# Four boundaries, the modulation sums and two early waits are rearranged in a two-block transformer kernel

## The reference

```python
# first block
x = x + 0.5 * swiglu(rmsnorm(x, ffn1_norm), ffn1_wgu, ffn1_wdown)          # f0
h = rmsnorm(x, mix_norm); z = h @ w_in
... # windowed attention, gated 31-tap causal convolution, merged, @ w_out
x = x + 0.5 * swiglu(rmsnorm(x, ffn2_norm), ffn2_wgu, ffn2_wdown)          # f1
e = rmsnorm(p @ ple_proj, ple_norm)
x = x + sigmoid(rmsnorm(x, ple_gate_norm) @ ple_gate_w) * e                # "gate", "emb"
# second block: nine modulation rows of 1024 from one vector c
mods = silu(c) @ w_ada + b_ada        # sh1, sc1, gt1, sh2, sc2, gt2, sh3, sc3, gt3
h = rmsnorm(x, g_pre[0]) * (1 + sc1) + sh1
x = x + 0.5 * gt1 * rmsnorm(swiglu(h, w_gu1, w_dn1), g_post[0])            # f2
h = rmsnorm(x, g_pre[1]) * (1 + sc2) + sh2
x = x + gt2 * rmsnorm(token_mixer(h), g_post[1])                           # mix2: GLA and forgetting attention
h = rmsnorm(x, g_pre[2]) * (1 + sc3) + sh3
x = x + 0.5 * gt3 * rmsnorm(swiglu(h, w_gu2, w_dn2), g_post[2])            # f3
```

## Time and profile before

| | |
|---|---|
| Time, median of 3 runs | 1416.35 us (1415.77 to 1418.84) |
| The profiled execution | 1407.82 us, its span 1406.0 us |
| Mean granted TensorE clock | 0.997 |
| PE busy | 1365.9 us, 97% of the span |
| DVE, ACT, POOL busy | 913.2, 742.9 and 57.8 us |

### The profile page before, as it was taken

One profiled execution on the slowest core, in us unless ns is written; L12 is line 12 of the kernel. 1 busy time (PEld: TensorE's weight loads), 2 busy tenths in 40 slices (PEclk: granted clock), 3 DMA queues, 4 the chain that ended last, 5 costly groups with the idle time before them and its releaser, 6 DMA issues.

```text
span 1406.0 us, 16993 instructions
## 1 busy us (share of the span) xinstructions
PE 1365.9 (97%) x6534; PEld 1127.1 (80%) x6534; DVE 913.2 (65%) x1309; ACT 742.9 (53%) x1144; POOL 57.8 (4%) x112
## 2 busy tenths in 40 slices
PE   7999999999999999999999999999999999899997
PEld 5888787878888888788688878688888888688886
DVE  5767747857466767666677774667776456755543
ACT  5544447556674544345754444766456563744442
POOL 3001000000000010000001000000000000000000
PEclk9999999999999999999999999999999999999999
DMA  9888756543257788765488875656453355456662
GB/s 296 280 264 279 224 177 187 175 130 91 90 179 237 224 275 275 268 216 159 145 259 270 266 247 174 184 153 177 143 156 91 105 162 170 147 180 187 188 184 85
DMA packets 166992, 270.68 MB, mean 193 GB/s; under 512 B 14178, under 2 KB 114698, under 8 KB 166912
## 3 DMA queue, kind: packets, MB, share of 16 engines
q1 hardware_dynamic: 154240, 226.66, 51.9%
q0 software_dynamic: 12368, 42.58, 9.1%
q10 hardware_dynamic: 304, 0.35, 0.1%
HBM read 268.50 MB, written 1.05 MB: 192 GB/s over the span
## 4 chain that ended last, share of the span: by engine, by line
PE 85%; DVE 5%; DMA 4%; ACT 4%; issue 1%; SPq 0%; DVEq 0%; ACTq 0%
PE ps L1769 26%; PE ps L1748 15%; PE ps L1750 15%; PE ps L1749 15%; DVE w_lo L1044 3%; DMA raw<-in_ffn_wgu_dram 2%; PE ps L1924 1%; ACT w_hi L573 1%; PE ps L2220 1%; DMA raw<-in_ffn_wdown_dram 1%; ACT shift L625 1%; PE ps L1836 1%; PE ps L1818 1%; PE ps L1960 1%; PE ps L1820 1%
## 5 line engine op out<-in xcount | busy, mean ns | idle before, releaser
L1044 DVE TENSOR_TENSOR w_lo<-raw,w_hi 128x1024 fp32r<-128x1024 f32 (+2 forms) x431 | 515.5, 1215 | 290.8 <-ACT w_hi L573 289.0
L573 ACT ACTIVATE w_hi<-raw 128x1024 fp32r<-128x1024 f32 (+2 forms) x431 | 447.8, 1054 | 334.4 <-DMA raw<-in_ffn_wgu_dram 95.1
L1748 PE MATMUL ps<-w_hi,a_hi 128*128 128x512 f32 (+1 forms) x1056 | 424.4, 402 | 1.9 <-DVE w_lo L1044 1.3
L1750 PE MATMUL ps<-w_hi,a_lo 128*128 128x512 f32 (+1 forms) x1056 | 411.9, 390 | 0.0
L1749 PE MATMUL ps<-w_lo,a_hi 128*128 128x512 f32 (+1 forms) x1056 | 411.1, 389 | 0.0
L1750 PEld LDWEIGHTS ps<-w_hi,a_lo 128*128 128x128 f32 x1056 | 199.1, 189 | 42.7
L1748 PEld LDWEIGHTS ps<-w_hi,a_hi 128*128 128x128 f32 x1056 | 199.5, 189 | 41.4 <-DVE w_lo L1044 2.7
L1749 PEld LDWEIGHTS ps<-w_lo,a_hi 128*128 128x128 f32 x1056 | 199.8, 189 | 37.8
L1769 PE MATMUL ps<-w_hi,hid_hi 128*128 128x512 f32 x336 | 105.1, 394 | 0.0
L1769 PE MATMUL ps<-w_lo,hid_hi 128*128 128x512 f32 x336 | 104.0, 391 | 0.0
L1769 PE MATMUL ps<-w_hi,hid_lo 128*128 128x512 f32 x336 | 104.0, 391 | 0.0
(11 more groups left out here) (380 smaller groups left out, 1389.8 us busy)
## 6 DMA issues: line engine op xcount, KB each, us to landing
raw<-in_ffn_wgu_dram SPq DMA_DIRECT2D x176, 256.0 KB, 4.4
raw<-in_w_in_dram SPq DMA_DIRECT2D x88, 512.0 KB, 3.7
raw<-in_w_gu_dram SPq DMA_DIRECT2D x176, 256.0 KB, 3.4
ada<-in_w_ada_dram POOLq DMA_DIRECT2D x72, 512.0 KB, 5.3
raw<-in_ffn_wdown_dram SPq DMA_DIRECT2D x44, 512.0 KB, 4.0
raw<-in_w_dn_dram SPq DMA_DIRECT2D x44, 512.0 KB, 3.6
raw<-in_w_in_dram SPq DMA_DIRECT2D x36, 256.0 KB, 3.0
raw<-in_w_out_dram SPq DMA_DIRECT2D x16, 512.0 KB, 3.5
```

Of the source, the lines that this page charges most:

```text
L573: act.activation(w_hi[:, u % RING, 0:nk * n], raw[:, u % RING, 0:nk * n], ACT.Copy).then_inc(hi_ready, 1)
L1044: dve.tensor_tensor(w_lo[:, u % RING, 0:nk * n], raw[:, u % RING, 0:nk * n], w_hi[:, u % RING, 0:nk * n].bitcast(F32), ALU.subtract).then_ ...
L1748: pe.matmul(dst(t)[:, 0:n], a[0], slot(u, w_hi, kk, n), start=kc == 0, stop=False)
L1750: i = pe.matmul(dst(t)[:, 0:n], a[1], slot(u, w_hi, kk, n), start=False, stop=kc == KC - 1)
```

## The change

- **Modulation sums.** DVE first transposes `acc_m` in blocks of 32x32 into two PSUM banks and reduces it to 128 x 32 (`fold_mods`, after blocks 4 and 8 of f0, f1 and f2); PE then makes one matmul of 32 columns with a new constant table (`C_SUM`) after the fourth unit of blocks 5 and 9. DVE takes the result one block later, in four pieces of 32 partitions.
- **Tile 0 at the boundaries.** POOL makes the high parts (`tile_hi` in its list), chunks 0 and 1 alone and then pairs; DVE makes the low parts of chunks 0 and 1 alone (`chunk_lo`). In tile 1 ACT makes the high parts of chunks 0 and 1 alone.
- **Second tile gated ahead.** At the boundaries to mix2 and f3 DVE does the two `gated` of tile 1 before the root of tile 0's norm, and ACT's square of tile 1 waits for them.
- **Boundary to f2.** Two weight units are split after the sigmoid of tile 0 instead of before it, on ACT and on DVE; the sum of tile 1 goes between low parts; `busy` has 10 matmuls instead of 20.
- **Last tile by halves.** The last two units of f3 are multiplied first into the one half of tile 1, then into the other; squares and gate products are made by halves.
- **Taps and GLA.** The last two tap matmuls move from step 10 to step 12. The 12 value matmuls of the GLA move into the middle of the next weight unit.

```diff
--- before.py
+++ after.py
...
-C_ID, C_ONES, C_TRI, C_D, C_W, C_COS, C_SIN, C_GLA = 0, 128, 256, 384, 512, 640, 656, 672
+C_ID, C_ONES, C_TRI, C_D, C_W, C_COS, C_SIN, C_SUM, C_GLA = 0, 128, 256, 384, 512, 640, 656, 672, 800
...
     s, q = i[:, None], i[None, :]
+    t[:, C_SUM:C_SUM + P] = s % 32 == q % 32
...
 epsb = keep("epsb", [P, 3])
+half_ss = keep("half_ss", [P, 2])
...
+    def tile_hi(key):
+        g = MODS[key]
+        for c, n in ((0, 1), (1, 1), (2, 2), (4, 2), (6, 2)):
+            pool.wait_ge(sem("shifted"), KC * T * g + c + n)
+            pool.tensor_copy(a_hi[:, c:c + n, 0:P], shift[:, c:c + n, :]).then_inc(sem("first_hi" if c == 0 else "act_hi"), 1)
...
     load_brow(2)
+    tile_hi("f2")
     load_ada(2 * ADA_F + 3, 3 * ADA_F)
+    tile_hi("mix2")
     pool.dma_start(ggla[:, :], A["g_gla_2"][0].partition_broadcast(P)).then_inc(sem("glam_landed"), 16)
+    tile_hi("f3")
...
                     act.activation(shift[:, k, :], turn_to(key, t, k), ACT.Identity, scale=modA[:, g, k:k + 1], bias=modB[:, g, k:k + 1])                               .then_inc(sem("shifted"), 1)
+                    if t == 1 and c == 0:
+                        act.wait_ge(sem("shifted"), KC * (T * g + t) + k + 1)
+                        act.activation(dst[:, k, :], shift[:, k, :], ACT.Copy).then_inc(sem("first_hi" if k == 0 else "act_hi"), 1)
+                if t == 0 or c == 0:
+                    continue
...
         act.wait_ge(used, end)
+        act.wait_ge(sem("post_made"), 4 * POST[prev])
...
     act.wait_ge(sem("rstd_ready"), NORM["gate"] + 1)
-    w.to(u_pg + KC + 2)
     act.activation(st[:, 0, 0, 0:T], rstd[:, :], ACT.Sigmoid)
+    w.to(u_pg + KC)
     act.activation(h[:, 0, :], behind(0), ACT.Sigmoid, scale=rstd[:, 0:1]).then_inc(sem("gate_ready"), 1)
+    w.to(u_pg + KC + 2)
...
     ffn_part(3)
-    for t in range(T):
...
-        post_tile("f3", t)
+    act.wait_ge(sem("first_tile"), FIRST_TILE["f3"])
+    post_tile("f3", 0)
+    act.wait_ge(sem("first_tile"), FIRST_TILE["f3"] + 1)
+    act.activation(junk[:, 0:512], acc(1, 0), ACT.Square, accum_out=half_ss[:, 0:1]).then_inc(sem("ss_ready"), 1)
+    act.wait_ge(used, ffn[3][1] + FC)
+    act.activation(junk[:, 512:], acc(1, 1), ACT.Square, accum_out=pss[:, 1:2]).then_inc(sem("pss_ready"), 1)
+    act.wait_ge(sem("pss_ready"), 2 * POST["f3"] + 2)
+    act.wait_ge(sem("emb_ready"), T + 1)
+    act.activation(rt[:, 1, 1:2], pss[:, 1:2], ACT.Sqrt, scale=1.0 / D, bias=half_ss[:, 1:2]).then_inc(sem("sqrt_ready"), 1)
...
+    def chunk_lo(key, t, c):
+        if c == 0:
+            dve.wait_ge(sem("first_hi"), T * MODS[key] + t + 1)
+        else:
+            dve.wait_ge(sem("act_hi"), 8 * TURN[key] + 4 * t + 1)
+        dst, hf = (v[:, c, t * P:(t + 1) * P] for v in (a_lo, a_hi))
+        dve.tensor_tensor(dst, shift[:, c, :], hf.bitcast(F32), ALU.subtract).then_inc(sem("first_lo" if c == 0 else "act_lo"), 1)
...
-    def post_and_norm(prev, key):
+    def post_and_norm(prev, key, end):
...
         post_sum(prev, 0, 1)
+        dve.wait_ge(used, end)
+        gated(prev, 1, 0)
+        gated(prev, 1, 1)
         normalise(key, 0)
-        dve.wait_ge(sem("pss_ready"), 2 * POST[prev] + 2)
-        gated(prev, 1, 0)
-        gated(prev, 1, 1)
-        tile_lo(key, 0, 0, 2)
         post_root(prev, 1)
+        chunk_lo(key, 0, 0)
+        post_sum(prev, 1, 0)
+        chunk_lo(key, 0, 1)
         tile_lo(key, 0, 2, 4)
-        post_sum(prev, 1, 0)
         normalise(key, 1)
-        tile_lo(key, 1)
+        chunk_lo(key, 1, 0)
+        chunk_lo(key, 1, 1)
+        tile_lo(key, 1, 2)
...
                 hidden_lo(f, j - 1)
-            take_mods(FFN[f], j)
+            take_mods(FFN[f], j - 1)
...
             i.then_inc(sem("hid_ready"), 1)
+            if f < 3 and j in (4, 8):
+                fold_mods(3 * f + j // 4 - 1)
...
+    def fold_mods(m):
+        dve.wait_ge(sem("ada_used"), KC * (m + 1))
+        blocks_ = ps[:, 6:8, :].rearrange("p b n -> p (b n)")
+        then(dve.transpose(blocks_, acc_m[:, m % 2, :]))
+        dve.tensor_reduce(rs36[:, 0:32], blocks_.rearrange("p (b n) -> p b n", n=32), AX, ALU.add).then_inc(sem("mod_folded"), 1)
...
             g, kind = m // 3, m % 3
-            if kind == 0:
...
+            if kind < 2:
+                for q in range(4):
+                    r = slice(32 * q, 32 * (q + 1))
+                    src = ps[r, 6, 0:32].rearrange("p (c q) -> p c q", q=4)[:, :, q]
+                    i = dve.tensor_tensor((modB, modA)[kind][r, g, :], src, par[r, :, ROW[("b_ada_2", m)]], ALU.add)
+            if kind == 1:
                 r = ROW[("g_pre_2", g)]
-                then(dve.tensor_tensor(modA[:, g, :], ps[:, 6, 0:KC], par[:, :, ROW[("b_ada_2", m)]], ALU.add))
+                then(i)
                 i = dve.scalar_tensor_tensor(modA[:, g, :], modA[:, g, :], 1.0, par[:, :, r], ALU.add, ALU.mult)
-            else:
+            elif kind == 2:
...
         dve.scalar_tensor_tensor(emb[:, t, :], wide(t), prs[:, t:t + 1], grow[:, :], ALU.mult, ALU.mult).then_inc(sem("emb_ready"), 1)
-    w.to(u_pg + KC + 2)
+    w.to(u_pg + KC)
         then(dve.tensor_tensor(h[:, t, :], h[:, t, :], emb[:, t, :], ALU.mult))
+    def emb_sum(t):
     gate_emb(0)
+    emb_sum(0)
+    w.to(u_pg + KC + 1)
     normalise("f2", 0)
-    tile_lo("f2", 0, 0, 2)
     gate_emb(1)
-    tile_lo("f2", 0, 2)
+    chunk_lo("f2", 0, 0)
+    chunk_lo("f2", 0, 1)
+    emb_sum(1)
+    tile_lo("f2", 0, 2, 4)
+    w.to(u_pg + KC + 2)
+    tile_lo("f2", 0, 4)
     normalise("f2", 1)
-    tile_lo("f2", 1)
+    chunk_lo("f2", 1, 0)
+    chunk_lo("f2", 1, 1)
+    tile_lo("f2", 1, 2)
     ffn_part(2)
-    post_and_norm("f2", "mix2")
+    post_and_norm("f2", "mix2", ffn[2][1] + FC)
...
     w.to(u_wo2 + KC + 2)
-    post_and_norm("mix2", "f3")
+    post_and_norm("mix2", "f3", u_wo2 + KC)
     ffn_part(3)
-    for t in range(T):
...
+    dve.wait_ge(sem("pss_ready"), 2 * POST["f3"] + 1)
+    gated("f3", 0, 0)
...
+    dve.wait_ge(sem("ss_ready"), 2 * len(NORM) + 1)
+    dve.tensor_scalar(half_ss[:, 1:2], half_ss[:, 0:1], 1.0 / D, EPS, ALU.mult, ALU.add).then_inc(sem("emb_ready"), 1)
+    gated("f3", 1, 0)
+    dve.wait_ge(sem("pss_ready"), 2 * POST["f3"] + 2)
+    gated("f3", 1, 1)
...
+    dve.wait_ge(sem("emb_ready"), T + 1)
+    then(dve.scalar_tensor_tensor(v, pss[:, 1:2], 1.0 / D, half_ss[:, 1:2], ALU.mult, ALU.add))
+    dve.wait_ge(sem("sqrt_ready"), ROOTS.index("f3_post1") + 1)
...
+    post_sum("f3", 1, 0)
+    post_sum("f3", 1, 1)
...
-    def last_rows(u0, n, hi, lo, bank=0, late=None):
+    def row_quarter(u, kc, t, half, last, hi, lo):
+        a = [v[:, kc, t * P:(t + 1) * P] for v in (hi, lo)]
+        for x_, w_ in ((0, w_hi), (0, w_lo), (1, w_hi)):
+            i = pe.matmul(acc(t, half), a[x_], slot(u, w_, 0, D, 512 * half, 512 * (half + 1)), start=False, stop=kc == last and x_ == 1)
+        return i
+    def last_rows(u0, n, hi, lo, bank=0, late=None, halves=False):
         i.then_inc(sem("first_tile"), 1)
+        if halves:
...
+            for half in range(2):
+                for k in range(n - 2, n):
+                    i = row_quarter(u0 + k, k, 1, half, n - 1, hi, lo)
+                    if half == 1:
+                        i.then_inc(used, 1)
+                if half == 0:
+                    i.then_inc(sem("first_tile"), 1)
+            return
...
         n = group(key)
-        pe.wait_ge(sem("act_lo"), 8 * TURN[key] + 4 * t + (kc // n + 1) * n // 2)
+        if key in MODS and kc == 0:
+            pe.wait_ge(sem("first_lo"), T * MODS[key] + t + 1)
+        else:
+            pe.wait_ge(sem("act_lo"), 8 * TURN[key] + 4 * t + (kc // n + 1) * n // 2)
...
                         turn_hidden(f, j - 1)
+                if i == 3:
...
         pe.wait_ge(sem("hid_lo_ready"), f * UPB + UPB)
-        last_rows(dn, FC, hid_hi, hid_lo, late=late)
+        last_rows(dn, FC, hid_hi, hid_lo, late=late, halves=f == 3)
...
             if m % 3 < 2:
-                pe.wait_ge(sem("ada_used"), KC * (m + 1))
+                pe.wait_ge(sem("mod_folded"), 2 * (m // 3) + m % 3 + 1)
...
             else:
-                for c in range(KC):
-                    i = pe.matmul(ps[:, 6, c:c + 1], acc_m[:, m % 2, c * P:(c + 1) * P], ones[:, 0:1], start=True, stop=True)
+                i = pe.matmul(ps[:, 6, 0:32], const[:, C_SUM:C_SUM + P], rs36[:, 0:32], start=True, stop=True)
...
-    def tap_spectrum():
+    def tap_spectrum(ks):
         pe.wait_ge(sem("table_lo"), 4)
-        for k in range(6):
+        for k in ks:
...
         if step == 10:
-            tap_spectrum()
+            tap_spectrum(range(4))
+        if step == 12:
+            tap_spectrum(range(4, 6))
...
     pe.wait_ge(sem("emb_ready"), T)
-    busy(20, 0)
+    busy(10, 0)
...
-    pe.wait_ge(sem("gla_masked"), NSTEP)
-    pe.wait_ge(sem("qkb_dve"), 8)
...
-        ins.then_inc(sem("gla_out"), 1)
+    def gla_values():
+        pe.wait_ge(sem("gla_masked"), NSTEP)
```

(4 more changed lines are left out.)

41 lines of the change are left out of this document (20 added, 21 removed).

## The result

The changed kernel took 1389.38 us (median of 4 executions, 1388.33 to 1393.01) and the kernel before 1416.06 (4 executions, 1412.47 to 1418.84, three of them those of the table ahead of the prediction): ratio 0.9847, 95% interval 0.9819 to 0.9876. The forecast was 1400.4, range 1395 to 1409. The profiled execution of the changed kernel took 1388.33, its span 1386.5.

What follows compares the result with a forecast made beforehand. PE, busy 97% of the span, was taken to bound the kernel. Terms of 7.4 + 2.6 + 3.0 + 0.8 + 0.95 + 0.5 + 1.0 - 0.2 = 16.0 us, taken off the median 1416.35, gave 1400.4, range 1395 to 1409.

Steps and rivals of the forecast that it cites:

- the last sentence of the sum: Whole kernel: the 16 us saved on the profiled span also come off the median of runs, 1416.35, giving 1400.4.
- sums: Three feed-forward parts: each first modulation sum saves 1.47 us, each second 1.0; 7.4 in all, ends 3.0 and 8.8.
- taps: Mixer: PE's 2.6 us wait for ACT to empty two banks goes; 2.6 gained, ends 0.7 and 3.2.
- table: Kernel start: loading the new 64 KB constant table in the crowded start loses 0.2 us.
- GLA: Second mixer's value matmuls: six matmuls cover PE's wait for banks that ACT's copies free; 0.5 us gained.
- a rival where longer waits bring a drop: Second sums give nothing or less: PE waits longer for `hid`, perhaps with a clock drop; 1405 to 1407, chance 0.15.
- boundary f2: Boundary to f2: earlier sigmoid and turn, fewer idle matmuls, single first chunk; 3.0 us gained, ends 1.5 and 3.8.
- boundary mix2: Boundary to mix2: tile 0's root 0.8 late, but tile 1's turn earlier; 0.8 us gained, ends -0.8 and 1.8.
- boundary f3: Boundary to f3: tile 1's turn 1.2 earlier, ACT's single copies give 0.25 back; 0.95 us gained, ends 0 and 2.
- end: Kernel end: half a square and one `gated` leave the chain; 1.0 us gained with the handover.
- the rival's mechanism: Boundaries: POOL's copies and DVE's two-source low parts hinder each other, so boundaries give nothing; 4.75 us go, 1405, chance 0.17.
- better than that: Whole kernel: faster than the forecast's 1397 to 1404, with all second sums whole and taps whole; chance 0.06.

Runs made afterwards that it cites:

- taps alone: The kernel before with only the last two tap matmuls moved from step 10 to step 12: 1405.95 us, ratio 0.9969.

## Why the prediction missed

**The step that failed** is the last sentence of the sum: "the median of the runs, 1416.35, is 8.5 above it, and from it I take the same 16". The 16.0 us were right: at equal clock it is 16.3 +- 0.8, and for an execution of the changed kernel at the profile's clock of 0.997 the text has 1391.8, where three such executions average 1391.7. In part that sum is luck, for errors of its terms cancel: sums, taps and table came 1.3 to 1.6 better, the boundaries and the GLA 0.8 worse. But the 8.5 us between the profile and the median were carried over to the changed kernel as a constant. Its 20 executions average 1391.4, which is 0.4 under those 1391.8; the 63 of before average 1411.4, only 3.6 above its profile. So 4.9 of the 8.5 were a high draw of the first executions of before. The other 3.6 are what before's mean clock of 0.9941 costs against the 0.997 of its profile (0.0029 at 1.23 per 0.001), and the changed kernel, at 0.9971, does not pay them. All four medians of the changed kernel, 1387.83 to 1393.76, lie under the range's lower end.

The first comparison's 26.7 are 16.3 at equal clock; 3.7 by the mean clocks over all executions (0.0030, at 1.23 per 0.001); 4.7 because the first series of before (1416.1) ran above its mean over all series (1411.4); and 2.0 because the changed kernel's (1389.4) ran below its own (1391.4). Whether the clock made the 4.7 too is not shown: no clock is on record for that series, and the line reaches 1416.4 only at 0.990, the lowest clock of the 63. Why the series of one kernel differ is not shown either.

The prediction saw the clock only on its bad side, in a rival where longer waits bring a drop. It had the other side in its own rows, 0.98 in the second window, but read it as standing behind the wait at the end of f1. That window ends at 590.00, before this wait; its stretch at half clock, 520.0 to 523.4, stands behind the first sum of f1.

**Term by term**, forecast and measured in us:

| term | forecast | measured | from |
|---|---|---|---|
| sums | 7.4 | 8.4 | 9.2 of PE's list, 0.8 back in waits, that less sure |
| taps | 2.6 | 2.7 to 3.0 | taps alone; three profiles |
| boundary f2 | 3.0 | 2.81 | start of the idle matmuls to the 60th load from the turn of tile 1 |
| boundary mix2 | 0.8 | 0.76 | same |
| boundary f3 | 0.95 | 0.69 | same |
| GLA | 0.5 | 0.15 | -0.65, then +0.5 |
| end | 1.0 | 1.0 | last weight load to end |
| table | -0.2 | not seen | the first `hid` begins between 30.6 and 31.9 without it, 30.7 and 32.3 with it |

- **Sums.** In f2, from the turn of block 0 to `first_down`'s second half without its last wait, it is 113.0 us in all four profiles with the old sums and no idle matmuls, and 109.8 to 109.9 in eleven with the new: 3.07 for two sums, 1.53 each, where 1.47 was worked out and only 1.0 granted for the second. The wait for the last `hid`, which was to grow by half a microsecond a part, is, for f0, f1 and f2 together, 6.4 us on the mean of the four and 7.3 on that of the seven that leave these waits as they are. The transfer behind block 9 does start earlier, and DVE's queue does hold 0.85 more; both effects are smaller than the spread of those sums (4.5 to 7.6 and 4.9 to 9.5) and of a single wait from one execution to the next (1.5, 2.4, 3.4 and 3.8 in f0 of the same changed kernel). Of the terms of the 16.0 this one is the most off, by 1.0, because the second sums came whole.
- **Taps** and **boundaries** came as worked out; the boundaries repeat within 0.06 us in all ten profiles that have them unedited, with the new sums and without, save one value at f3 (0.55). That the idle matmuls end just in time held (0.18 of wait).
- **GpSimd.** The copies were to take 0.25 and 0.35. A single chunk took 0.30 with VectorE idle beside it, a pair 0.40 where it began ahead of VectorE's instruction, and 0.90 to 1.04 where VectorE's sum into `x` ran beside it for 0.64 to 0.78 us. The low parts of a pair took 0.48 to 0.65 beside a copy and 0.42 without. So the rival's mechanism is there, on both sides. The Trainium skill ("GPSIMD Engine Reference", 1. Specifications) says that the two engines share their SBUF interfaces, with contention when VectorE reads two SBUF inputs. The trace agrees: the sums into `x` and the low parts both read two. It did not decide, because the copies still keep pace with ScalarE's shifts: the first product comes 0.1 to 0.2 us later than with ScalarE's copies, and tile 1 comes 0.7 to 1.2 earlier.
- **The rivals.** None of the priced ones came; the result lies in "better than that", which had 0.06, and mostly for other reasons than the text gives there: all second sums whole is part of it (1.0), but the high anchor and the clock are the larger ones. That it lies below the range by 5.6 us and not by less is in part the draw of the first comparison.
- **GLA.** The wait for `AT` went, and DVE's maximum for the next heads, which had been done in its shadow, became late by 0.5.

## What to carry to other kernels

A saving read from one profile is a saving at that execution's clock: compare it with executions at the same granted clock, and do not carry the distance between one profile and the median over to another kernel. Count separately the waits that a change takes from TensorE: lengthened waits cost 1.4 to 1.5 times themselves here. Before a helper engine is judged by its own durations, look at whom it relieves: GpSimd's copies slowed VectorE's low parts and still brought 3.1 us. When a wait ends with a queue of several instructions in front of the one that is wanted, move what is not due yet, but follow what was moved to its own reader, which here cost as much until it was moved too.

## What the runs showed of the hardware

- A wait of TensorE of 0.56 to 2.9 us with sixteen one-column records behind it was followed by a stretch at 1.2 GHz in five profiles of five. Waits of 0.57 to 2.5 us at the same place with full matmuls behind them were not, in ten of ten, and the sixteen records without such a wait in one place of 25.
- Lengthening three waits of TensorE by 6.7 us together lowered the mean granted clock from 0.9962 to 0.9932 and cost 9.2 us between the means.
- GpSimd's conversion of 128x256 took 0.40 where it began ahead of VectorE's instruction (ScalarE's took 0.42), and up to 1.04 beside VectorE's sum of two inputs; VectorE's low part of a pair beside it took up to 0.65 instead of 0.42.
- VectorE's transpose by 32x32 blocks, 128x1024 from SBUF into PSUM, took 1.25 us, and the reduction of 128x1024 from PSUM to 128x32 took 1.22.
- The same kernel on the same chip spreads by 10 us and more (1404.88 to 1419.63), and most of the spread goes with the granted clock (1.23 us for each 0.001, 1.9 of scatter).
